# Gated linear heads: row sums and mean squares from rounded parts, the mean product two steps later

## The reference, cut to what matters

```python
s = jnp.einsum('bhtd,bhsd->bhts', qc, kc) * jnp.exp(log_d - m_t[..., None])
num = jnp.einsum('bhts,bhsd->bhtd', s, vc) + ...
den = jnp.sum(s, axis=-1) + ...
h = num / jnp.maximum(jnp.abs(den), jnp.exp(-m_t))[..., None]
...
h_ml = _rmsnorm(h_ml, ml_g_out[l])     # h * rsqrt(mean(h*h) + EPS) * g
y_ml = jax.nn.sigmoid(ml_o) * h_ml
```

## Time and profile before

| | us |
|---|---|
| median of 3 runs | 2027.15 |
| lowest, highest | 2026.24, 2029.54 |
| span of the profiled execution, first to last instruction | 2026.0 |

### The profile page before, as it was taken

The page is one execution under the profiler, slowest core; times in us unless marked ns, Lnnn a source line. Parts: engine busy times, 40 slices in busy tenths (PEclk is TensorE's granted clock), DMA queues, the critical chain, the costliest instruction groups (busy, mean ns, idle before and its releaser), DMA issues.

```text
span 2026.0 us, 31822 instructions
## 1 busy us (share of the span) xinstructions
PE 2000.9 (99%) x12918; PEld 1608.2 (79%) x12918; DVE 1455.5 (72%) x2281; ACT 584.3 (29%) x1013; POOL 353.2 (17%) x317
## 2 busy tenths in 40 slices
PE   9999999999999999999999999999999999999999
PEld 7888888887777777777888877777888888888887
DVE  6666666667867777678997877576566769849973
ACT  2000122222655454434873233533210010000000
POOL 2121111111110110011112212111112212222221
PEclk9999999999999999999999999999999999999999
DMA  5323322222211121122222323111223323322232
GB/s 184 102 90 99 100 84 78 94 84 75 85 64 54 64 70 58 65 84 84 63 73 84 126 78 99 42 63 48 78 83 94 107 91 104 104 94 94 94 99 89
DMA packets 53361, 173.52 MB, mean 86 GB/s; under 512 B 6464, under 2 KB 6720, under 8 KB 53088
## 3 DMA queue, kind: packets, MB, share of 16 engines
q1 hardware_dynamic: 48112, 161.46, 24.2%
q10 hardware_dynamic: 5104, 10.03, 1.9%
HBM read 169.30 MB, written 2.16 MB: 85 GB/s over the span
## 4 chain that ended last, share of the span: by engine, by line
PE 85%; DVE 9%; ACT 4%; issue 2%; DMA 1%; ACTq 0%; DVEq 0%; SPq 0%
PE ps_lin L1934 24%; PE ps_lin L1936 23%; PE ps_lin L1935 23%; PE ps_att L1983 7%; PE ps_aux L1983 4%; DVE arena L436 3%; ACT arena L1362 2%; DVE arena L430 2%; PE ps_att L1992 1%; DVE w_lo L430 1%; ACT L1368 1%; DVE arena L433 1%; PE ps_lin L1954 1%; PE ps_lin L1956 0%; PE ps_lin L1955 0%
## 5 line engine op out<-in xcount | busy, mean ns | idle before, releaser
L1934 PE MATMUL ps_lin<-xw_hi,w_hi 128*128 128x512 f32 x1704 | 689.9, 405 | 1.2 <-issue 0.6
L1936 PE MATMUL ps_lin<-xw_hi,w_lo 128*128 128x512 f32 x1704 | 665.6, 391 | 0.0
L1935 PE MATMUL ps_lin<-xw_lo,w_hi 128*128 128x512 f32 x1704 | 664.8, 390 | 0.0
L412 POOL TENSOR_SCALAR w_hi<-raw 128x1024 fp32r<-128x1024 f32 (+2 forms) x309 | 348.8, 1129 | 1655.3 <-PE ps_lin L1936 1537.3
L1362 ACT ACTIVATE arena<-arena 128x512 f32<-128x512 f32 (+7 forms) x331 | 206.4, 630 | 750.2 <-DVE arena L430 361.4
L430 DVE TENSOR_TENSOR w_lo<-raw,w_hi 128x1024 fp32r<-128x1024 f32 (+2 forms) x340 | 376.6, 1110 | 45.5 <-POOL w_hi L412 16.9
L1934 PEld LDWEIGHTS ps_lin<-xw_hi,w_hi 128*128 128x128 f32 x1704 | 320.6, 188 | 68.5 <-issue 4.3
L1936 PEld LDWEIGHTS ps_lin<-xw_hi,w_lo 128*128 128x128 f32 x1704 | 320.1, 188 | 68.6
L1935 PEld LDWEIGHTS ps_lin<-xw_lo,w_hi 128*128 128x128 f32 x1704 | 320.9, 188 | 59.3 <-issue 0.5
L430 DVE TENSOR_TENSOR arena<-ps_lin,rstd 128x512 f32<-128x512 f32 (+3 forms) x220 | 147.6, 671 | 182.4 <-PE ps_lin L1936 173.9
L1934 PE MATMUL ps_lin<-y_hi,w_hi 128*128 128x512 f32 (+1 forms) x544 | 205.2, 377 | 0.0
(11 more groups left out here) (188 smaller groups left out, 1697.2 us busy)
## 6 DMA issues: line engine op xcount, KB each, us to landing
raw<-in_w_up SPq DMA_DIRECT2D x44, 512.0 KB, 3.3
raw<-in_conv_w_in SPq DMA_DIRECT2D x32, 512.0 KB, 3.3
raw<-in_fox_w_in SPq DMA_DIRECT2D x32, 512.0 KB, 3.3
raw<-in_gdn_w_in SPq DMA_DIRECT2D x32, 512.0 KB, 3.3
raw<-in_w_gate SPq DMA_DIRECT2D x24, 512.0 KB, 3.3
raw<-in_swa_w_in SPq DMA_DIRECT2D x20, 512.0 KB, 3.3
raw<-in_w_ml SPq DMA_DIRECT2D x16, 512.0 KB, 4.0
raw<-in_w_down SPq DMA_DIRECT2D x16, 512.0 KB, 3.5
```

The costliest lines, as they stand in the source:

```text
L412: pool.tensor_scalar(w_whole(n, kc * c)[0], w_raw(n, kc * c), 1.0, 0.0, mult, add).then_inc(s("w_rounded"), 1)
L1934: pe.matmul(o, wh, hi, start=first and k == 0, stop=False)
L1935: pe.matmul(o, wh, lo, start=False, stop=False)
L1936: ins = pe.matmul(o, wl, hi, start=False, stop=last and k == kc - 1)
```

## The change

The sum of scores and the mean of squares become two float32r products of 512 columns each: a rounded part and the low part, which DVE subtracts. ACT makes the rounded score sums by two copies and the rounded squares by a second Square; both use rows of `y_hi` and `y_lo` that are free there. The matrices of ones and of 1/128 are set by two more memsets on POOL at the start. In part 3 of turns 1 to 3, two of the eight steps of the next tile (`project(2)`) go ahead of the mean product; `tile()` behind it makes the remaining six. Two counters become one (`gate_act`) and `gdn_kd` is counted on `gdn_vb`.

```diff
+        ml_ones, ml_mean = sb("ml_ones", [P, P], f32r), sb("ml_mean", [P, P], f32r)
+        ml_sq, ml_col = (y_hi[:, 0, :], y_lo[:, 0, :]), (y_hi[:, 1, :], y_lo[:, 1, :])
...
             pool.memset(v_tmp[:, 0:P], 1.0 / D).then_inc(s("mean_set"), 1)
+            pool.memset(ml_ones[:].bitcast(f32), 1.0).then_inc(s("mean_set"), 1)
+            pool.memset(ml_mean[:].bitcast(f32), 1.0 / P).then_inc(s("mean_set"), 1)
...
-            dve.wait_ge(s("gdn_tanh"), 1)
+            dve.wait_ge(s("gate_act"), 3)
...
-                tt(chunks(F["kd"]), chunks(ps_att[:, 1, :]), column(2, h), mult).then_inc(s("gdn_kd"), 1)
+                tt(chunks(F["kd"]), chunks(ps_att[:, 1, :]), column(2, h), mult).then_inc(s("gdn_vb"), 1)
...
+                        if part == 1:
+                            dve.wait_ge(s("ml_col"), h + 1)
+                            tt(ml_col[1][:, 0:P], F["ST"][:, 0:P], ml_col[0][:, 0:P].bitcast(f32), sub)
+                            tt(ml_col[1][:, P:], F["sums"][:, P:], ml_col[0][:, P:].bitcast(f32), sub).then_inc(s("ml_low"), 1)
                         if part in (1, 2) and r == ML_H:
                             sb_tile(part - 1, 0)
+                        if part == 3:
+                            dve.wait_ge(s("ml_sq"), h + 1)
+                            tt(ml_sq[1], sq[:, 0, :], ml_sq[0].bitcast(f32), sub).then_inc(s("ml_low"), 1)
                         if part == 3 and r == ML_H:
...
+                            act.wait_ge(s("ml_sums"), (NT - 1) * (h + 1))
+                            activation(ml_col[0][:, 0:P], F["ST"][:, 0:P], ACT.Copy)
+                            activation(ml_col[0][:, P:], F["sums"][:, P:], ACT.Copy).then_inc(s("ml_col"), 1)
                             act.wait_ge(s("v_turned"), VT["ml"] + h + 1)
...
-                            activation(sq[:, 0, :], F["t2"], ACT.Square).then_inc(s("ml_sq"), 1)
+                            activation(sq[:, 0, :], F["t2"], ACT.Square)
+                            activation(ml_sq[0], F["t2"], ACT.Square).then_inc(s("ml_sq"), 1)
...
-                            pe.wait_ge(s("ml_sums"), (NT - 1) * (h + 1))
-                            mm(ps_att[:, 1, 0:P], mat("ones"), F["ST"][:, 0:P], True, False)
-                            mm(ps_att[:, 1, P:], mat("ones"), F["sums"][:, P:], False, True).then_inc(s("ml_pv"), 1)
+                            pe.wait_ge(s("mean_set"), 3)
+                            pe.wait_ge(s("ml_low"), 2 * h + 1)
+                            mm(ps_att[:, 1, :], ml_ones[:], ml_col[0], True, False)
+                            mm(ps_att[:, 1, :], ml_ones[:], ml_col[1], False, True).then_inc(s("ml_pv"), 1)
...
                         if part == 3:
+                            if r < ML_H:
+                                project(2)
                             pe.wait_ge(*aux("ml_rn", h + 1))
-                            pe.wait_ge(s("ml_sq"), h + 1)
-                            mm_last(ps_aux[:], mat("mean_h"), sq[:, 0, :]).then_inc(s("ml_ss"), 1)
+                            pe.wait_ge(s("ml_low"), 2 * h + 2)
+                            mm(ps_aux[:], ml_mean[:], ml_sq[0], True, False)
+                            mm(ps_aux[:], ml_mean[:], ml_sq[1], False, True).then_inc(s("ml_ss"), 1)
```

More of the change, by code:

```diff
@@ L619, in _ @@
             dve.wait_ge(s("softplus_in"), made("softplus_in"))
-            dve.wait_ge(s("softplus_out"), 1)
+            dve.wait_ge(s("gate_act"), 1)
             step(stt(F["r1"][0:8, :], F["r1"][0:8, :], 0.0, F["ab"][0:8, :], mn, sub))
@@ L740, in _ @@
             weights(tile_of("gdn_w_gates", 0))
-            dve.wait_ge(s("softplus_out"), 2)
+            dve.wait_ge(s("gate_act"), 2)
             step(stt(F["r2"][R8, :], F["r2"][R8, :], 0.0, F["r3"][R8, :], mx, add))
@@ L802, in gdn_head @@
                 step(tt(chunks(F["kbg"]), chunks(ps_att[:, 1, :]), column(1, h), mult))
-                tt(chunks(F["kd"]), chunks(ps_att[:, 1, :]), column(2, h), mult).then_inc(s("gdn_kd"), 1)
+                tt(chunks(F["kd"]), chunks(ps_att[:, 1, :]), column(2, h), mult).then_inc(s("gdn_vb"), 1)
                 dve.wait_ge(s("gdn_tok"), 2 * h + 2)
                 tt(chunks(F["vb"]), chunks(ps_att[:, 2, :]), column(0, h), mult).then_inc(s("gdn_vb"), 1)
-                dve.wait_ge(s("gdn_vb"), h + 1)
+                dve.wait_ge(s("gdn_vb"), 2 * h + 2)
                 if 0 < h < GDN_H - 1:
@@ L1086, in _ @@
             dve.wait_ge(s("softplus_in"), made("softplus_in"))
-            dve.wait_ge(s("softplus_out"), 3)
+            dve.wait_ge(s("gate_act"), 4)
             step(stt(F["r1"][R4, :], F["r1"][R4, :], 0.0, F["em"][R4, :], mn, sub))
@@ L1445, in _ @@
             step(activation(F["ab"][0:8, :], F["ab"][0:8, :], ACT.Exp, scale=-1.0))
-            activation(F["ab"][0:8, :], F["ab"][0:8, :], ACT.Ln, bias=1.0).then_inc(s("softplus_out"), 1)
-            act.wait_ge(s("softplus_out"), made("softplus_out"))
+            activation(F["ab"][0:8, :], F["ab"][0:8, :], ACT.Ln, bias=1.0).then_inc(s("gate_act"), 1)
+            act.wait_ge(s("gate_act"), made("gate_act"))
             def fox_row(h):
@@ L1490, in _ @@
             step(activation(F["r3"][R8, :], F["r3"][R8, :], ACT.Exp, scale=-1.0))
-            activation(F["r3"][R8, :], F["r3"][R8, :], ACT.Ln, bias=1.0).then_inc(s("softplus_out"), 1)
-            act.wait_ge(s("softplus_out"), made("softplus_out"))
+            activation(F["r3"][R8, :], F["r3"][R8, :], ACT.Ln, bias=1.0).then_inc(s("gate_act"), 1)
+            act.wait_ge(s("gate_act"), made("gate_act"))
             use(ACT.Tanh)
             act.wait_ge(bank_read(tile_of("gdn_w_gates", 0)), reads(tile_of("gdn_w_gates", 0)))
-            activation(F["r1"][R8, :], F["r1"][R8, :], ACT.Tanh, scale=0.5).then_inc(s("gdn_tanh"), 1)
+            activation(F["r1"][R8, :], F["r1"][R8, :], ACT.Tanh, scale=0.5).then_inc(s("gate_act"), 1)
+            made("gate_act")
             def gdn_rows_G(h):
@@ L1744, in _ @@
             step(activation(F["em"][R4, :], F["em"][R4, :], ACT.Exp, scale=-1.0))
-            activation(F["em"][R4, :], F["em"][R4, :], ACT.Ln, bias=1.0).then_inc(s("softplus_out"), 1)
-            act.wait_ge(s("softplus_out"), made("softplus_out"))
+            activation(F["em"][R4, :], F["em"][R4, :], ACT.Ln, bias=1.0).then_inc(s("gate_act"), 1)
+            act.wait_ge(s("gate_act"), made("gate_act"))
             for g in range(2):
@@ L2144, in gdn_head @@
                 four(X, lambda c: blk(k_, c), B("kb")).then_inc(s("gdn_A"), 1)
-                pe.wait_ge(s("gdn_kd"), h + 1)
+                pe.wait_ge(s("gdn_vb"), 2 * h + 1)
                 four(Y, lambda c: blk(k_, c), lambda c: blk(q_, c)).then_inc(s("gdn_A"), 1)
                 fill(GDN_FILL["U0"])
-                pe.wait_ge(s("gdn_vb"), h + 1)
+                pe.wait_ge(s("gdn_vb"), 2 * h + 2)
                 fill(1)
```

## The result

The median of seven runs after the change is 2031.89 us (2031.17 to 2035.19), against 2026.24 us (2025.67 to 2029.54) in seven runs of the kernel before: +5.65 us, a ratio of 1.0025 [1.0014, 1.0036] (in brackets, here and below, the 95% interval of the ratio). The kernel became slower.

A forecast was written before the change was run, and what follows sets the result against it. It took the DVE-ACT chain from convolution to mean product as the bound: low-part delays and half-clock losses, less TensorE's savings, net +5.6, took the span from 2026.0 to 2031.6; plus 1.15 around it, 2032.8 us, range 2029.5 to 2036.0.

The forecast's parts named there:

- The rival that TensorE sets the end: Low parts ready when TensorE comes, so it keeps its savings: 2020.9 us, or 2024.0 with waits as now; chance 0.10.
- The time around the span: Run time outside the traced span: 1.15 us carried over, taking the forecast from 2031.6 to 2032.8.
- +5.6: Net growth of the span, 2026.0 to 2031.6 us, with head 1 restarting at full clock and head 2 at half.
- Head 0: First head: mean product from 1184.71 to 1187.44 (0.88 + 1.85), DVE's next step from 1187.66 to 1189.9, 1.36 late.
- Head 1: Second head: a further 0.73 + 1.85 us, so its mean product goes from 1215.85 to 1219.79.
- TensorE's savings: Cheaper products on TensorE: 0.42 us a head at the sum of scores, root 0.48 earlier after the mean's start.
- full, then half: Clock behind the mean products: full in head 1 after 2.8 us wait, half in head 2 after 4.0; net +5.6.
- +4.2 case: Clock rival: half behind head 1, full behind head 2, tile's end at 1256.4; 2031.4 us, chance 0.15.
- the signs that I named: Waits before the mean products of 3 to 4.5 us in heads 0 to 2; turns of 31.7 to 32.2 us.
- every head restart cold (+6.0): By the skill's clock rule, half clock behind the mean product in every head: net +6.0 us.
- GpSimd's collision: Rival: GpSimd's rounding stretches one VectorE subtraction a head by about 1.04 us; +8.7, 2035.9 us, chance 0.12.
- The 0 for the two steps: Two steps moved ahead of the mean product: 1.36 us before it instead of behind it, adding nothing.

The follow-up runs named there:

- e1: Kernel before with only the sum of scores from rounded parts, mean of squares left float32 and no steps ahead; 2028.75 us, +1.40.
- e4: Changed kernel with five steps of the next tile ahead of the mean product instead of two; 2032.96 us, +5.65 against before.
- e12: Changed kernel with four GpSimd roundings a turn held until VectorE reaches given rows; 2031.39 us, +4.14 against before.
- e11: Kernel before with two steps ahead of the float32 mean product and four GpSimd roundings a turn held for VectorE; 2023.26 us, -3.77.
- e6: Kernel before with two steps ahead of the mean product and VectorE's weights of k behind its convolution; 2026.97 us, -0.38.
- e7: Changed kernel with VectorE's weights of k moved behind its convolution; 2031.71 us, +4.40 against before.
- e9: Changed kernel with the low part of the squares ahead of the weights and evacuation of v; 2033.82 us, +6.8 against before.
- e2: Kernel before with only the mean of squares from rounded parts and its two steps ahead, sum of scores left float32; 2032.96 us, +5.61.
- e5: Kernel before with two steps of the next tile ahead of its float32 mean product, nothing else; 2028.18 us, +0.83.
- e10: Kernel before with two steps ahead, late weights of k and four GpSimd roundings a turn held for VectorE; 2023.29 us, -3.74.
- e3: Changed kernel with the two steps put back behind the mean product; 2037.92 us, +10.6 against before.

## Why the prediction was right

It forecast 2032.8 us, with slower as the likeliest; 2031.89 was measured. What set the time was read rightly; that the number came so near is in part luck. The span was forecast at 2031.6 and measured at 2030.1, 1.5 too long, and the time around it was taken 0.64 too short. Step by step:

- **DVE and ACT, not TensorE, set the turn.** Shown from several sides: TensorE's saved time turned into waits (`e1`, 7.3 us for 4.8); more steps ahead only moved the wait (`e4`); the rounded parts, in kernels that differ by nothing else, cost 7.9 us (`e12` against `e11`). The rival that TensorE sets the end is refuted. The runs that should have shown the chain by shortening or reordering it (`e6`, `e7`, `e9`) missed.
- **The time around the span.** I carried 1.15 us; it is 1.79 in the execution after. This 0.64 lies in the forecast of the time, not in the +5.6.
- **Head 0.** Mean product forecast at 1187.44, measured at 1187.26; DVE's step behind the root forecast at 1189.9, measured at 1189.78. In this head the two low parts did cost what the rows of before gave.
- **Head 1.** h was forecast 1.36 + 0.73 = 2.09 later than 1214.29, measured 1216.38, 2.09 later. The parts of it differ: DVE came 1.72 late to the evacuation of o (1194.65 for 1192.93; 0.48 of the wait for TensorE was left, where I had it gone), and lost only 0.37 more behind it. From h to the mean product I had 3.41 (1.56 + 1.85), measured 3.62: the weights at 1217.10 took 1.43 instead of 1.22, a rounding of GpSimd having started at 1216.41. Hence 1220.00 for 1219.79.
- **TensorE's savings.** The new sum of scores takes 1210.62 - 1210.08 = 0.54, so it saves 0.34 and not 0.42; the first of the two products is followed after 0.31 and not 0.23. The root: from the mean product to DVE's next step it took 2.49 us before (1215.85 to 1218.34) and takes 2.03 in head 2 after (1251.82 to 1253.85), the forecast gain of 0.48 within 0.02. But at half clock the distance is 2.52 (1220.00 to 1222.52): the gain is eaten where it was needed.
- **The clock: this step failed.** I took "full, then half" for heads 1 and 2, by the length of the waits: 2.8 in head 1 would stay at full clock, 4.0 in head 2 would not. The trace has "half, then full", with 2.40 at both. That was my +4.2 case, which gave 1256.4 for the end of head 2's tile; measured 1256.46, and the spans differ by 4.1. So the path that was traced is the third case, and that the medians differ by 5.65 and not by 4.1 comes from the execution traced before, whose time was 1.55 above its median. That case I had given 0.15. My +5.6 met the medians by luck. Of the signs that I named, the waits before heads 1 and 2 stayed at 2.40, below 3 to 4.5, and the first turn (32.74) went above 32.2. The loss behind head 0 was larger too: products stood at 0.43 us spacing until 1192.52, 5.26 us where I had 3.9, and TensorE reached the next scores at 1194.45 and not at 1193.84.
- **The Trainium skill**, "TensorE: Matmul & The Clock Gate", section "HAM oscillation — how this bites in real kernels", as I used it in the prediction, would have had every head restart cold (+6.0). The trace agrees in heads 0 and 1 and differs in head 2 (2.40 us, PEclk 1.00). That use went beyond the section: the waits in its example are longer than 2.40 us, so it does not decide heads 1 and 2.
- **GpSimd's collision**, which I gave 0.12 and one subtraction a head, exists. In the rows read here it costs 0.56 to 0.84 where a rounding began at most 0.4 us ahead of a row or inside a group of rows, and 0.21 where it had run for 0.69 us (at 1217.10). It stands in the rows of `e2`, `e5`, `e6` and `e9`; only for `e5` and `e6` did a run take it away (`e11`, `e10`). I overlooked that the kernel before already has two such rows ahead of head 0 (1166.75 and 1173.66). In the traced execution of the change it took 0.21 in the first of the two turns and 0.04 in the second (1249.08); three rows are stretched in the third, by 2.28 in all, where no wait stands before head 3's mean product.
- **The 0 for the two steps** was right as work, but not as a move: they are worth 5 to 6 us to the change (`e3`), and shift GpSimd's rounding against DVE (`e5`).

What stays open: why one wait of 2.40 us is followed by half clock and another is not; how much of the 5.65 us is the chain and how much the clock; and which runs of a kernel have which pattern, since only one execution of each was traced. Not tried: the gates without the steps, so that the share of the two in the gain of `e11` is not shown, the gates with the rounded sum alone, and the low part of the squares on another engine.

## What to carry to other kernels

A product made cheaper by splitting its operand costs an engine the split; where that engine's chain up to the product sets the turn, as DVE's and ACT's did here, the cheaper product shows up as a longer wait on a TensorE that is 99% busy by the page. Follow what releases the longest wait before pricing the product. When work is moved on one engine, look also at which other engine's work starts on its events: two steps moved on TensorE gained nothing by themselves, because GpSimd's rounding moved with them; with the rounding held back the kernel was 3.8 us faster than before.

## What the hardware showed that was not expected

**Who starts first keeps its speed.** A rounding on GpSimd of 1.04 us that is under way when DVE's row begins lengthens that row, by 0.65 to 0.73 us in `e5` (1.94 for 1.22). The rounding itself takes 1.15 to 1.40 there; a row of DVE was running or just beginning at each of its starts. With DVE's row begun first, the row keeps its 1.22 and GpSimd takes 1.98 (`e11`). Holding GpSimd back was free in `e11`, where its result was not yet due.
The Trainium skill, "SBUF — State Buffer", section "SBUF: two separate sides", describes a port pair that VectorE and GpSimd share as a lock that whichever starts first keeps for its whole instruction while the other blocks, for VectorE's instructions with two SBUF inputs among others. These subtractions have two; the two traces agree, with 0.72 us lost on VectorE in the one order and 0.94 on GpSimd in the other.

**The same wait, two clocks.** After waits of 2.40 us the mean product restarted at half clock in head 1 and at full clock in head 2 of the same execution. In `e1` it waited 3.93 us and still started at full speed; the clock fell only behind it. Timeline of TensorE, `e1`:

```profile
1184.66 1.10 PE L1995 MATMUL ps_aux<-sq,mats 128*128 128x384 f32 x4 [3.93 <-ACT sq L1370]
```

and the stretches behind the first of them, `e1`:

```profile
1184.66:1188.50 3.84, 3.84 (x12) 3.01 (x13) 2.27 (x5) 1.36 (x3) 0.00 (x0) 0.69 0.57 183
1188.50:1192.00 3.50, 3.50 (x14) 2.77 (x14) 2.94 (x4) 0.50 (x1) 0.00 (x0) 0.86 0.06 23
```

In `e4`, behind waits of 2.41, 2.42 and 2.40 us, the clock was 1.00, 0.60 and 0.58 up to the next scores. So in these traces the length of the wait alone does not tell what the clock will be, and the price of a wait at the mean product lies, by my estimate, anywhere from nothing to some 2.6 us (half of the 5.26 us behind head 0).
